# Second FFN pass: the low part of the gated value computed on GpSimd instead of VectorE

## The chip, the cores and the metric

One NeuronCore of a Trainium2 chip runs the whole program. The metric is device time in microseconds (us). The kernel before took 2487.13 us, the median of three runs (2484.39 to 2489.68). A profiled execution of it took 2494.55 us; every row below is from that one, and times in the rows count from the start of its span of 2492.5 us.

The engines: TensorE (PE; its weight loads are PEld), VectorE (DVE), ScalarE (ACT), GpSimd (POOL), and SyncE (SP), which issues most of the transfers.

## The reference, cut to what matters

Two layers of a diffusion block on 1024 tokens of width 1024. The second layer's feed-forward network is where the change is:

```python
def _conv_ffn(h, w_in, conv_w, conv_b, w_out, grid):
    u, g = jnp.split(h @ w_in, 2, axis=-1)          # w_in: 1024 x (2 * 2816)
    g = _dwconv_grid(g, conv_w, conv_b, grid)       # 3x3 depthwise, tokens as a 16 x 64 grid
    return (jax.nn.silu(g) * u) @ w_out             # w_out: 2816 x 1024
...
    fx = _conv_ffn(_modulate(x, norm_g[i, 2], sh2, sc2), ffn_w_in[i], ffn_conv_w[i], ffn_conv_b[i], ffn_w_out[i], grid_x)
    x = x + gt2 * _rms_norm(fx, norm_g[i, 3])
```

## The kernel before, in words

**Precision.** Every float32 matrix product is made of three matmuls. Each operand is split into a high part (rounded to the format that TensorE takes, by ScalarE) and a low part (the value minus its high part, by GpSimd or VectorE): high x high, low x high, high x low. L717, L718 and L719 are such a triple, L1365 to L1367 another.

**The second pass.** The 2816 hidden channels are 22 tiles of 128, `j` = 0 to 21. For each tile TensorE makes seven products of 12 matmuls each, in the order `g1`, `s1`, `s2`, `s4`, `s3`, `g2`, `u2`: sums and differences of halves of the weights, from which gate and up value of all 1024 tokens are put together. VectorE and ScalarE combine them (`keep_a`, `keep_b`, L2843, L2849, L2854). VectorE then adds eight taps of the convolution (L2822), ScalarE applies silu, VectorE multiplies by the up value (`fprod`, L2829, function `f_gate`), ScalarE makes the high part `fa_hi` (L2130) and VectorE the low part `fa_lo` (L2835, function `f_low`). With them TensorE runs `down`: 16 triples (8 output blocks by 2 token halves), one each into one of three banks of PSUM in turn, and VectorE adds each to `y_x` (L2868, function `f_add`). Triple n waits until accumulation n-3 is done.

**The order.** Everything is written out by hand, one instruction stream per engine with semaphores between. TensorE: `products(j)`, then `down(j-1)`. VectorE, in `f_tile(j)`: taps of j-1, gate second half of j, gate product of j-1, up second half of j, low part of j-1, gate first half of j, accumulations of j-1. Tile 0 and 1 are written ahead of the loop, tiles 2 to 13 are a hardware loop, and 14 to 21 are unrolled. In tiles 14 to 19 VectorE also computes half a column of a modulation vector (`last_mod_half`, four instructions of 128x256 into `macc_x`, L2294 and L2297), right before the accumulations.

**GpSimd**, in `parts(j)`, splits the weights of the next tile: the low part of `g1` and of the output weights (`fw_lo`, L3061), the sums `s1`, `s2`, the low of `s1`, the sum `s4`, the lows of `s2` and `s4`, the sum `s3`, then the lows of `s3`, `g2` and `u2` (sums are L3047, lows L3055). When the last low is done, SyncE loads the next tile's weights into `f_raw`.

**The end.** The last tile has an `fa_hi2` of its own, and after its gate product no other work of VectorE lies in between.

Of the kernel before, what the change touches and what calls it, by code (L numbers as in the profile page):

```python
# [17 lines left out]
F32 = mybir.dt.float32  # L18
F32R = mybir.dt.float32r
ALU = mybir.AluOpType  # L20
# [10 lines left out]
FT = DFF // P  # L31
# [111 lines left out]
def build(nc, a):  # L143
    with ExitStack() as ctx:
        sems = {}

        def sem(name):
            if name not in sems:
                sems[name] = ctx.enter_context(nc.semaphore(name))
            return sems[name]  # L150
# [4 lines left out]
        def at(name, offset, shape, dt=F32):  # L155
            return nc.alloc_sbuf_tensor_at(name, shape, dt, offset=base + offset)
# [111 lines left out]
        fprod = at("fprod", WORK + 4096, [P, 2, TX])  # L268
        fa_lo = at("fa_lo", WORK + 4096, [P, 2, TX], F32R)
        keep_a = at("keep_a", WORK + 12288, [P, TH])  # L270
        keep_b = at("keep_b", WORK + 14336, [P, TH])
        fa_hi = at("fa_hi", WORK + 16384, [P, TX], F32R)
# [126 lines left out]
        def scaled_x(n, d):  # L399
# [4 lines left out]
        SECOND = {  # L404
            "tap_done": 8 * FT,
            "acc_ready": FT,
            "silu_done": FT,
            "a_done": FT,
            "a_hi_ready": FT,
            "a_lo_ready": FT,  # L410
            "y_part": 7 * FT,
            "w_out_used": 2 * FT + CREDIT,
# [1770 lines left out]
        def _(dve):  # L2183
# [103 lines left out]
            def last_mod_half(n):  # L2287

                c, h = FT - 1 + n // 2, n % 2
                out = macc_x[c - FT + 1][:]  # L2290
                dve.wait_ge(sem("modw1_in"), 16 * (FT + n))
                for k in range(KH * h, KH * h + KH):
                    if k == 0:
                        ins = dve.tensor_scalar(out, modh[:, 0, :], c_pad[:, 0, 0:1], None, ALU.mult)  # L2294
                    else:
                        dve.wait_ge(sem("mod_sum"), c * 16 + 2 * k)
                        ins = dve.scalar_tensor_tensor(out, modh[:, k % KH, :], c_pad[:, k, 0:1], out, ALU.mult, ALU.add)  # L2297
                    ins.then_inc(sem("mod_sum"), 2)
# [513 lines left out]
            def f_taps(j):  # L2812

                cv = fcv[:, j + FT, :]
                g, ac = grid(bank(BANK_G, TX), "x"), grid(acc[:], "x")
                dve.wait_ge(sem("acc_ready"), j + (SECOND["acc_ready"] + 1))
                for i, (r, c) in enumerate(p1.taps):
                    out, src = tap_views(ac, g, r, c, p1.R, p1.W)
                    if i:
                        dve.wait_ge(sem("tap_done"), j * 8 + (SECOND["tap_done"] + i))  # L2820
                    t = tap_index(r, c)
                    dve.scalar_tensor_tensor(out, src, cv[:, t:t + 1], out, ALU.mult, ALU.add).then_inc(sem("tap_done"), 1)  # L2822

            def f_gate(j, par):

                dve.wait_ge(sem("silu_done"), j + (SECOND["silu_done"] + 1))
                dve.wait_ge(sem("act_moved"), j * 4 + (SECOND["act_moved"] + 4))
                dve.wait_ge(sem("dve_moved"), j * 3 + (SECOND["dve_moved"] + 3))
                dve.tensor_tensor(fprod[:, par, :], acc[:], fprod[:, par, :], ALU.mult).then_inc(sem("a_done"), 1)  # L2829

            def f_low(j, par, last=False):

                dve.wait_ge(sem("a_hi_ready"), j + (SECOND["a_hi_ready"] + 1))
                hi = fa_hi2 if last else fa_hi
                dve.tensor_tensor(fa_lo[:, par, :], fprod[:, par, :], hi[:].bitcast(F32), ALU.subtract).then_inc(sem("a_lo_ready"), 1)  # L2835

            def gate_second(j, first=False):

                dve.wait_ge(sem("w_in_used"), j * 7 + (SECOND["w_in_used"] + done_at(first, "s4")))
                dve.wait_ge(sem("act_moved"), j * 4 + (SECOND["act_moved"] + 3))  # L2840
                if not first:
                    dve.wait_ge(sem("tap_done"), j * 8 + SECOND["tap_done"])
                dve.tensor_tensor(ps[:, BANK_G + 1, :], keep_b[:], ps[:, BANK_B, :], ALU.add).then_inc(sem("dve_moved"), 1)  # L2843

            def up_second(j, par, first=False):

                dve.wait_ge(sem("w_in_used"), j * 7 + (SECOND["w_in_used"] + done_at(first, "s3")))
                dve.wait_ge(sem("act_moved"), j * 4 + (SECOND["act_moved"] + 3))
                dve.tensor_tensor(fprod[:, par, TH:TX], fprod[:, par, TH:TX], ps[:, BANK_A, :], ALU.add).then_inc(sem("dve_moved"), 1)  # L2849

            def gate_first(j):

                dve.wait_ge(sem("w_in_used"), j * 7 + (SECOND["w_in_used"] + 6))
                dve.tensor_tensor(ps[:, BANK_G, :], keep_a[:], ps[:, BANK_C, :], ALU.add).then_inc(sem("dve_moved"), 1)  # L2854
# [16 lines left out]
            def f_tile(j, par, adds=True, mod_half=None):  # L2871

                f_taps(j - 1)
                gate_second(j)
                f_gate(j - 1, 1 - par)
                up_second(j, par)
                f_low(j - 1, 1 - par)
                gate_first(j)
                if mod_half is not None:
                    last_mod_half(mod_half)  # L2880
                if adds:
                    f_add(j - 1)
# [3 lines left out]
            gate_first(0)  # L2886
            f_taps(0)
            f_gate(0, 0)
            f_low(0, 0)
            gate_second(1)  # L2890
            up_second(1, 1)
            gate_first(1)
# [56 lines left out]
        def _(pool):  # L2949
# [57 lines left out]
            for u, (dr, n) in enumerate(units):  # L3007
                if n >= 2:
                    i = x_index[u]
# [7 lines left out]
                for v in ([u - 2] if u < len(units) - 1 else [u - 2, u - 1, u]):  # L3017
                    if v in sec_index:
                        i = sec_index[v]
# [12 lines left out]
            def part_sum(name, j, first=False):  # L3032

                if first and name == "s4":
                    pool.wait_ge(sem("r_p"), 4)
                if first and name == "s3":
                    pool.wait_ge(sem("r_q"), 4)
                if not first:
                    pool.wait_ge(sem("w_in_used"), j * 7 + (SECOND["w_in_used"] + free_at(name) - 7))
                one, two, op = {"s1": (part("u1"), part("u2"), ALU.add), "s2": (p_val["s1"][:], part("g1"), ALU.subtract),  # L3040
                                "s4": (part("g2"), p_val["s2"][:], ALU.subtract), "s3": (part("g1"), part("u1"), ALU.subtract)}[name]
                n = ("s1", "s2", "s4", "s3").index(name)
                if name == "s1":
                    pool.wait_ge(sem("raw_in0"), j * 16 + (SECOND["raw_in0"] + 16))
                else:
                    pool.wait_ge(sem("pool_added"), j * 4 + (SECOND["pool_added"] + n))
                pool.tensor_tensor(p_val[name][:], one, two, op).then_inc(sem("pool_added"), 1)  # L3047

            def part_low(name, j, first=False):

                pool.wait_ge(sem("hi_in"), j * 7 + (SECOND["hi_in"] + made_at(first, name)))
                if name in RAW_PART and not first:
                    pool.wait_ge(sem("w_in_used"), j * 7 + (SECOND["w_in_used"] + free_at(name) - 7))
                src = part(name) if name in RAW_PART else p_val[name][:]
                pool.tensor_tensor(p_lo[name][:], src, p_hi[name][:].bitcast(F32), ALU.subtract).then_inc(sem("lo_in"), 1)  # L3055

            def out_low(j, last=False):

                pool.wait_ge(sem("hi_out"), j + (SECOND["hi_out"] + 1))
                w = int(last)  # L3060
                pool.tensor_tensor(fw_lo[w][:], fw_raw[w][:], fw_hi[w][:].bitcast(F32), ALU.subtract).then_inc(sem("lo_out"), 1)  # L3061

            def parts(j, between=None):

                part_low("g1", j)
                if between is not None:
                    between()
                part_sum("s1", j)
                part_sum("s2", j)
                part_low("s1", j)  # L3070
                part_sum("s4", j)
                part_low("s2", j)
                part_low("s4", j)
                part_sum("s3", j)
                part_low("s3", j)
                part_low("g2", j)
                part_low("u2", j)
# [24 lines left out]
                pool.tensor_tensor(x_lo["t3"][:, k:k + 2, :], x_val["t3"][:, k:k + 2, :], x_hi["t3"][:, k:k + 2, :].bitcast(F32), ALU.subtract)\  # L3102
                    .then_inc(sem("pool_low"), 1)
            parts(1)
            parts(2, lambda: out_low(0))
            with pool.Fori(0, FT // 2 - 2) as i:
                parts(i * 2 + 3, lambda: out_low(i * 2 + 1))
                parts(i * 2 + 4, lambda: out_low(i * 2 + 2))
            parts(FT - 1, lambda: out_low(FT - 3))
            out_low(FT - 2)  # L3110
            out_low(FT - 1, True)

            def residual(h, d):
# [96 lines left out]
```

## Time and profile before

| | |
|---|---|
| median of three runs | 2487.13 us (2484.39 to 2489.68) |
| profiled execution, its own time | 2494.55 us |
| its span | 2492.5 us |
| mean granted TensorE clock | 0.976 |
| TensorE busy | 2354.7 us, 94% |
| VectorE busy | 1742.9 us, 70% |
| ScalarE busy | 815.7 us, 33% |
| GpSimd busy | 875.3 us, 35% |
| `fa_lo` on VectorE (L2835) | 22 instructions, median 2.286 us, 1.221 to 2.364 |

The busy shares are means over stages that have different limits. In the page's 40 slices VectorE stands at 8 to 9 tenths through the second FFN pass (from about 1785 us on), and TensorE at 9. A row of the timeline gives start, duration, engine, line, operation, output and inputs, how many instructions are merged, and in brackets how long the engine sat idle before and what ended that.

### The profile page before, as it was taken

Reading aid. Unit: us, or ns where it says so; the run is one execution under the profiler, and the core shown is the slowest. Engines: PE = TensorE matmul, PEld = TensorE weight load, DVE = VectorE, ACT = ScalarE, POOL = GpSimd, SP = SyncE. Lnnn points to the kernel's source line nnn. Section 1 sums busy time; section 2 is a strip of 40 time slices with the busy share of each in tenths; the row PEclk is TensorE's granted clock in tenths of the full one; section 3 lists DMA queues with packets and bytes.
Section 4 is the critical chain, followed back from the end, with each engine's and each line's share of the span. In section 5 each row is a group of like instructions: output and inputs, shape, how many; then the busy total and the mean of one; then the engine's idle time right before and its main releaser. Section 6 shows DMA issues by size and latency. Waiting matters only on the chain.

```text
span 2492.5 us, 36004 instructions
## 1 busy us (share of the span) xinstructions
PE 2354.7 (94%) x13606; PEld 1926.0 (77%) x13606; DVE 1742.9 (70%) x2193; ACT 815.7 (33%) x1182; POOL 875.3 (35%) x432
## 2 busy tenths in 40 slices
PE   7989999999999999999999989798599999999996
PEld 5557777787777778998889987676378888887784
DVE  4467888888888884553533326615778888899986
ACT  3641111121111226553442233323333333333332
POOL 0012122121221235662221115520555665655552
PEclk9999999999999999999999999899799999999998
DMA  8651211222112344552121258512111111111113
GB/s 348 221 195 76 84 51 75 84 84 84 52 74 84 118 173 162 198 178 102 60 79 62 70 140 232 145 34 87 66 48 54 50 50 50 50 59 67 67 42 135
DMA packets 106689, 255.08 MB, mean 102 GB/s; under 512 B 8929, under 2 KB 62817, under 8 KB 92129
## 3 DMA queue, kind: packets, MB, share of 16 engines
q1 hardware_dynamic: 89024, 228.56, 26.6%
q10 hardware_dynamic: 17568, 25.17, 2.8%
q8 instruction: 69, 1.13, 0.2%
q14 instruction: 28, 0.22, 0.0%
HBM read 223.68 MB, written 30.02 MB: 102 GB/s over the span
## 4 chain that ended last, share of the span: by engine, by line
PE 78%; DVE 12%; ACT 4%; DMA 3%; issue 2%; POOL 1%; SPq 0%; ACTq 0%; DVEq 0%; POOLq 0%
PE ps L717 17%; PE ps L718 16%; PE ps L719 16%; PE ps L1365 4%; PE ps L1367 4%; PE ps L1366 4%; DVE acc L2822 3%; DVE y_x L2868 2%; PE ps L1115 2%; PE ps L1116 2%; PE ps L1117 2%; PE ps L1268 1%; PE ps L819 1%; PE ps L852 1%; PE ps L754 1%
## 5 line engine op out<-in xcount | busy, mean ns | idle before, releaser
L2953 POOL TENSOR_TENSOR w_lo<-raw,w_hi 128x2048 fp32r<-128x2048 f32 x57 | 266.8, 4681 | 653.0 <-ACT w_hi L1604 293.9
L717 PE MATMUL ps<-hx_hi,w_hi 128*128 128x512 f32 x848 | 338.7, 399 | 2.5 <-ACT mix_out_c L1758 1.0
L718 PE MATMUL ps<-hx_hi,w_lo 128*128 128x512 f32 x848 | 331.8, 391 | 0.0
L719 PE MATMUL ps<-hx_lo,w_hi 128*128 128x512 f32 x848 | 331.5, 391 | 0.0
L2333 DVE TENSOR_TENSOR y_x<-y_x,ps 128x1024 f32<-128x1024 f32 x176 | 214.7, 1221 | 63.0 <-PE ps L719 59.5
L2315 DVE SCALAR_TENSOR_TENSOR acc<-ps,fcv,acc 128x945 f32<-128x945 f32 (+2 forms) x176 | 215.0, 1222 | 37.4 <-ACT acc L1648 16.3
L2822 DVE SCALAR_TENSOR_TENSOR acc<-ps,fcv,acc 128x945 f32<-128x945 f32 (+2 forms) x176 | 215.0, 1222 | 18.6 <-ACT acc L2159 2.7
L2868 DVE TENSOR_TENSOR y_x<-y_x,ps 128x512 f32<-128x512 f32 x304 | 205.2, 687 | 14.1 <-PE ps L719 14.0
L717 PEld LDWEIGHTS ps<-hx_hi,w_hi 128*128 128x128 f32 x848 | 160.2, 189 | 40.3 <-DVE hx_lo L2470 2.5
L719 PEld LDWEIGHTS ps<-hx_lo,w_hi 128*128 128x128 f32 x848 | 160.1, 189 | 34.0
L718 PEld LDWEIGHTS ps<-hx_hi,w_lo 128*128 128x128 f32 x848 | 160.3, 189 | 30.6
L2964 POOL TENSOR_TENSOR a_lo<-prod,a_hi 128x1024 fp32r<-128x1024 f32 x22 | 52.9, 2404 | 318.7 <-ACT a_hi L1666 318.7
L2284 DVE SCALAR_TENSOR_TENSOR macc<-modw,c_pad,macc 128x256 f32<-128x256 f32 x280 | 155.5, 627 | 0.0
L717 PE MATMUL ps<-fa_hi,fw_hi 128*128 128x512 f32 x352 | 140.1, 398 | 15.4 <-DVE y_x L2868 7.9
L3055 POOL TENSOR_TENSOR p_s_lo<-p_s_val,p_s_hi 128x512 fp32r<-128x512 f32 x88 | 140.6, 1608 | 30.8 <-ACT p_s_hi L2028 30.8
L1115 PE MATMUL ps<-w_hi,hx_hi 128*128 128x256 f32 x512 | 145.4, 284 | 4.3 <-ACT stage L1885 4.3
L717 PE MATMUL ps<-a_hi,w_hi 128*128 128x512 f32 x352 | 145.5, 413 | 2.5 <-DVE y_x L2333 1.2
L1116 PE MATMUL ps<-w_lo,hx_hi 128*128 128x256 f32 x512 | 144.9, 283 | 0.0
L1117 PE MATMUL ps<-w_hi,hx_lo 128*128 128x256 f32 x512 | 144.8, 283 | 0.0
L719 PE MATMUL ps<-a_lo,w_hi 128*128 128x512 f32 x352 | 138.1, 392 | 0.0
L718 PE MATMUL ps<-a_hi,w_lo 128*128 128x512 f32 x352 | 138.0, 392 | 0.0
L718 PE MATMUL ps<-fa_hi,fw_lo 128*128 128x512 f32 x352 | 137.8, 391 | 0.0
(379 smaller groups left out, 5668.7 us busy)
## 6 DMA issues: line engine op xcount, KB each, us to landing
raw<-in_ffn_w SPq DMA_DIRECT2D x44, 1024.0 KB, 6.6
modw<-in_modw SPq DMA_DIRECT2D x48, 512.0 KB, 7.3
raw<-in_ffn_w SPq DMA_DIRECT2D x44, 512.0 KB, 6.4
f_raw<-in_ffn_w SPq DMA_DIRECT2D x22, 1024.0 KB, 5.0
modw<-in_modw SPq DMA_DIRECT2D x21, 1024.0 KB, 4.8
raw<-in_mlstm_w SPq DMA_DIRECT2D x14, 1024.0 KB, 5.3
fw_raw<-in_ffn_w SPq DMA_DIRECT2D x22, 512.0 KB, 3.7
vch<-v_scr SPq DMA_DIRECT2D x18, 512.0 KB, 4.5
```

What stands on the lines that cost most here:

```text
L717: pe.matmul(out, whi, hhi, start=first, stop=False)
L718: pe.matmul(out, wlo, hhi, start=False, stop=False)
L719: return pe.matmul(out, whi, hlo, start=False, stop=last)
L1115: pe.matmul(out, hi[:, k, t0:t0 + CH], wcol(0, k, 0, 2), start=first, stop=False)
L1116: pe.matmul(out, hi[:, k, t0:t0 + CH], wcol(1, k, 0, 2), start=False, stop=False)
L1117: return pe.matmul(out, lo[:, k, t0:t0 + CH], wcol(0, k, 0, 2), start=False, stop=last)
L2284: ins = dve.scalar_tensor_tensor(macc[:, x, :], modw1[:, k, :], c_pad[:, k, x:x + 1], macc[:, x, :], ALU.mult, ALU.add)
L2315: dve.scalar_tensor_tensor(out, src, cv[:, t:t + 1], out, ALU.mult, ALU.add).then_inc(sem("tap_done"), 1)
L2333: dve.tensor_tensor(y[:, d, :], y[:, d, :], bank(4 + 2 * (d % 2), p.T), ALU.add).then_inc(sem("y_added"), 1)
L2822: dve.scalar_tensor_tensor(out, src, cv[:, t:t + 1], out, ALU.mult, ALU.add).then_inc(sem("tap_done"), 1)
L2868: ins = dve.tensor_tensor(y, y, ps[:, BANK_Y + n % 3, :], ALU.add)
L2953: pool.tensor_tensor(w_lo[:, slot, 0:2048], raw[:, slot, 0:2048], w_hi[:, slot, 0:2048].bitcast(F32), ALU.subtract)\
```

## The change

The subtraction that makes `fa_lo` moves from VectorE's stream into GpSimd's for tiles 0 to 20. It stands there between the sum `s4` and the low of `s2`. For the last tile VectorE keeps it, with one more wait, for GpSimd's part of tile 20.

```diff
             def f_low(j, par, last=False):
 
                 dve.wait_ge(sem("a_hi_ready"), j + (SECOND["a_hi_ready"] + 1))
+                dve.wait_ge(sem("a_lo_ready"), j + SECOND["a_lo_ready"])
...
                 f_gate(j - 1, 1 - par)
                 up_second(j, par)
-                f_low(j - 1, 1 - par)
                 gate_first(j)
...
             f_gate(0, 0)
-            f_low(0, 0)
             gate_second(1)
...
+            def gated_low(j, par):
+
+                pool.wait_ge(sem("a_hi_ready"), j + (SECOND["a_hi_ready"] + 1))
+                pool.tensor_tensor(fa_lo[:, par, :], fprod[:, par, :], fa_hi[:].bitcast(F32), ALU.subtract).then_inc(sem("a_lo_ready"), 1)
+
+            def parts(j, between=None, gated=None):
...
                 part_sum("s4", j)
+                if gated is not None:
+                    gated()
                 part_low("s2", j)
...
-            parts(2, lambda: out_low(0))
+            parts(2, lambda: out_low(0), lambda: gated_low(0, 0))
             with pool.Fori(0, FT // 2 - 2) as i:
-                parts(i * 2 + 3, lambda: out_low(i * 2 + 1))
-                parts(i * 2 + 4, lambda: out_low(i * 2 + 2))
-            parts(FT - 1, lambda: out_low(FT - 3))
+                parts(i * 2 + 3, lambda: out_low(i * 2 + 1), lambda: gated_low(i * 2 + 1, 1))
+                parts(i * 2 + 4, lambda: out_low(i * 2 + 2), lambda: gated_low(i * 2 + 2, 0))
+            parts(FT - 1, lambda: out_low(FT - 3), lambda: gated_low(FT - 3, 1))
             out_low(FT - 2)
+            gated_low(FT - 2, 0)
             out_low(FT - 1, True)
```

VectorE ahead of the loop, from the gate product of tile 0 to the accumulations of tile 0. Before:

```order
L2829 TENSOR_TENSOR fprod_202<-acc_84,fprod_202 128x1024
L2835 TENSOR_TENSOR fa_lo_203<-fprod_202,fa_hi_206 128x1024
L2843 TENSOR_TENSOR ps<-keep_b_205,ps 128x512
L2849 TENSOR_TENSOR fprod_202<-fprod_202,ps 128x512
L2854 TENSOR_TENSOR ps<-keep_a_204,ps 128x512
L2866 COPY y_x_51<-ps 128x512 x16
```

The same place on VectorE in the changed kernel:

```order
L2829 TENSOR_TENSOR fprod_202<-acc_84,fprod_202 128x1024
L2844 TENSOR_TENSOR ps<-keep_b_205,ps 128x512
L2850 TENSOR_TENSOR fprod_202<-fprod_202,ps 128x512
L2855 TENSOR_TENSOR ps<-keep_a_204,ps 128x512
L2867 COPY y_x_51<-ps 128x512 x16
```

Three half-size instructions move ahead by one large one (line numbers are one higher in the changed kernel).

VectorE in tile 14, the first with a modulation half. Before:

```order
L2829 TENSOR_TENSOR fprod_202<-acc_84,fprod_202 128x1024
L2849 TENSOR_TENSOR fprod_202<-fprod_202,ps 128x512
L2835 TENSOR_TENSOR fa_lo_203<-fprod_202,fa_hi_206 128x1024
L2854 TENSOR_TENSOR ps<-keep_a_204,ps 128x512
L2294 TENSOR_SCALAR macc_x0_90<-modh_208,c_pad_220 128x256
L2297 SCALAR_TENSOR_TENSOR macc_x0_90<-modh_208,c_pad_220,macc_x0_90 128x256 x3
L2868 TENSOR_TENSOR y_x_51<-y_x_51,ps 128x512 x16
```

The same place on VectorE in the changed kernel:

```order
L2829 TENSOR_TENSOR fprod_202<-acc_84,fprod_202 128x1024
L2850 TENSOR_TENSOR fprod_202<-fprod_202,ps 128x512
L2855 TENSOR_TENSOR ps<-keep_a_204,ps 128x512
L2294 TENSOR_SCALAR macc_x0_90<-modh_208,c_pad_220 128x256
L2297 SCALAR_TENSOR_TENSOR macc_x0_90<-modh_208,c_pad_220,macc_x0_90 128x256 x3
L2869 TENSOR_TENSOR y_x_51<-y_x_51,ps 128x512 x16
```

Between the up value and the modulation half one instruction is left on VectorE, where there were two.

GpSimd in the last `parts`, which is the order of every tile from 2 on. Before:

```order
L3047 TENSOR_TENSOR p_s2_val_200<-p_s1_val_196,f_raw_201 128x512
L3055 TENSOR_TENSOR p_s1_lo_189<-p_s1_val_196,p_s1_hi_182 128x512
L3047 TENSOR_TENSOR p_s4_val_197<-f_raw_201,p_s2_val_200 128x512
L3055 TENSOR_TENSOR p_s2_lo_193<-p_s2_val_200,p_s2_hi_186 128x512
L3055 TENSOR_TENSOR p_s4_lo_190<-p_s4_val_197,p_s4_hi_183 128x512
```

The same place on GpSimd in the changed kernel:

```order
L3046 TENSOR_TENSOR p_s2_val_200<-p_s1_val_196,f_raw_201 128x512
L3054 TENSOR_TENSOR p_s1_lo_189<-p_s1_val_196,p_s1_hi_182 128x512
L3046 TENSOR_TENSOR p_s4_val_197<-f_raw_201,p_s2_val_200 128x512
L3065 TENSOR_TENSOR fa_lo_203<-fprod_202,fa_hi_206 128x1024
L3054 TENSOR_TENSOR p_s2_lo_193<-p_s2_val_200,p_s2_hi_186 128x512
L3054 TENSOR_TENSOR p_s4_lo_190<-p_s4_val_197,p_s4_hi_183 128x512
```

The low of `s2` and all that follows it on GpSimd now stands behind `fa_lo`, and so behind ScalarE's `fa_hi`.

## Rows read from the trace of the kernel before

**Rows 1.** The page, part 1: busy time by engine.

```profile
PE 2354.7 (94%) x13606; PEld 1926.0 (77%) x13606; DVE 1742.9 (70%) x2193; ACT 815.7 (33%) x1182; POOL 875.3 (35%) x432
```

**Rows 2.** Timeline of VectorE and TensorE, one tile of the loop.

```profile
2033.04 2.28 DVE L2835 TENSOR_TENSOR fa_lo<-fprod,fa_hi 128x1024 fp32r<-128x1024 f32 x1 [0.61 <-ACT fa_hi L2130]
...
2036.91 10.89 DVE L2868 TENSOR_TENSOR y_x<-y_x,ps 128x512 f32<-128x512 f32 x16 [0.99 <-PE ps L719]
...
2036.04 0.39 PE L717 MATMUL ps<-fa_hi,fw_hi 128*128 128x512 f32 x1
```

**Rows 3.** Timeline of GpSimd, the same tile and the next.

```profile
2030.92 2.07 POOL L3047 TENSOR_TENSOR p_s_val<-f_raw,p_s_val 128x512 f32<-128x512 f32 x1 [0.17 <-PE ps L1367]
...
2051.20 1.31 POOL L3055 TENSOR_TENSOR p_g_lo<-f_raw,p_g_hi 128x512 fp32r<-128x512 f32 x1 [8.83 <-ACT p_g_hi L2028]
```

**Rows 4.** Instructions of lines 3061 and 2284: duration in ns, least, median, greatest.

```profile
L3061 POOL TENSOR_TENSOR fw_lo<-fw_raw,fw_hi x22: 2369/2412/2428, 1808.1 to 2439.5; 128x1024 fp32r<-128x1024 f32 x22
...
L2284 DVE SCALAR_TENSOR_TENSOR macc<-modw,c_pad,macc x280: 465/474/2631, 224.4 to 889.5; 128x256 f32<-128x256 f32 x140
```

**Rows 5.** Timeline of VectorE, GpSimd and TensorE in tile 15.

```profile
2243.61 2.29 DVE L2835 TENSOR_TENSOR fa_lo<-fprod,fa_hi 128x1024 fp32r<-128x1024 f32 x1 [0.31 <-ACT fa_hi L2130]
...
2246.42 4.37 DVE L2297 SCALAR_TENSOR_TENSOR macc_x<-modh,c_pad,macc_x 128x256 f32<-128x256 f32 x4
2250.70 10.59 DVE L2868 TENSOR_TENSOR y_x<-y_x,ps 128x512 f32<-128x512 f32 x16
...
2243.52 1.29 POOL L3047 TENSOR_TENSOR p_s_val<-f_raw,p_s_val 128x512 f32<-128x512 f32 x1
2244.77 3.71 POOL L3055 TENSOR_TENSOR p_s_lo<-p_s_val,p_s_hi 128x512 fp32r<-128x512 f32 x2
...
2247.85 0.39 PE L717 MATMUL ps<-fa_hi,fw_hi 128*128 128x512 f32 x1
```

**Rows 6.** TensorE's waits, 2190 to 2390 us: sum, times, longest (us).

```profile
PE ps L717 <- DVE y_x L2868: 7.9, 6, 1.4
```

**Rows 7.** Timeline of VectorE: accumulations of the loop's last tile and of tile 20.

```profile
2187.08 3.41 DVE L2868 TENSOR_TENSOR y_x<-y_x,ps 128x512 f32<-128x512 f32 x5 [0.97 <-PE ps L719]
...
2407.15 10.89 DVE L2868 TENSOR_TENSOR y_x<-y_x,ps 128x512 f32<-128x512 f32 x16 [2.31 <-PE ps L719]
```

**Rows 8.** Timeline of VectorE, GpSimd and TensorE in tile 1, ahead of the loop.

```profile
1814.78 1.80 DVE L2829 TENSOR_TENSOR fprod<-acc,fprod 128x1024 f32<-128x1024 f32 x1 [10.07 <-ACT acc L2123]
...
1815.73 2.01 POOL L3047 TENSOR_TENSOR p_s_val<-f_raw,p_s_val 128x512 f32<-128x512 f32 x1 [0.22 <-PE ps L1367]
...
1817.97 0.39 PE L1367 MATMUL ps<-x_lo,p_g_hi 128*128 128x512 f32 x1
1821.31 0.50 PE L1365 MATMUL ps<-t_hi,p_u_hi 128*128 128x512 f32 x1 [2.94 <-DVE fprod L2849]
...
1824.70 0.63 PE L1366 MATMUL ps<-t_hi,p_u_lo 128*128 128x512 f32 x1
```

**Rows 9.** Timeline of VectorE and GpSimd at 571 us, in the first pass.

```profile
571.51 2.62 DVE L2284 SCALAR_TENSOR_TENSOR macc<-modw,c_pad,macc 128x256 f32<-128x256 f32 x1
...
571.45 2.40 POOL L2964 TENSOR_TENSOR a_lo<-prod,a_hi 128x1024 fp32r<-128x1024 f32 x1 [13.46 <-ACT a_hi L1666]
```

**Rows 10.** Timeline of TensorE: the first matmul behind each of two stalls.

```profile
1148.17 0.36 PE L1115 MATMUL ps<-w_hi,hx_hi 128*128 128x256 f32 x1 [2.06 <-ACT stage L1885]
...
1507.10 0.38 PE L1268 MATMUL ps<-vch,dmat 128*128 128x129 f32 x1 [2.03 <-DMA vch<-v_scr]
```

**Rows 11.** Busy time by engine in short stretches; PEclk is behind the five engines.

```profile
1148.20:1152.00 3.80, 3.80 (x32) 3.80 (x33) 0.00 (x0) 1.18 (x4) 2.77 (x1) 1.00 0.37 113
...
1509.00:1511.00 2.00, 2.00 (x16) 1.77 (x16) 0.00 (x0) 0.00 (x0) 0.16 (x1) 0.50 1.04 272
...
1823.00:1825.50 2.50, 2.50 (x7) 1.98 (x6) 0.00 (x0) 0.10 (x1) 0.00 (x0) 0.50 0.00 0
...
2251.00:2256.00 5.00, 4.56 (x20) 3.80 (x21) 5.00 (x9) 0.69 (x2) 3.52 (x3) 1.00 0.11 21
```

More of the change, by code:

```diff
@@ L3061, in out_low @@
                 pool.tensor_tensor(fw_lo[w][:], fw_raw[w][:], fw_hi[w][:].bitcast(F32), ALU.subtract).then_inc(sem("lo_out"), 1)
-            def parts(j, between=None):
+            def gated_low(j, par):
+                pool.wait_ge(sem("a_hi_ready"), j + (SECOND["a_hi_ready"] + 1))
+                pool.tensor_tensor(fa_lo[:, par, :], fprod[:, par, :], fa_hi[:].bitcast(F32), ALU.subtract).then_inc(sem("a_lo_ready"), 1)
+            def parts(j, between=None, gated=None):
                 part_low("g1", j)
```

## The prediction

> **What bounds the kernel now.** I read the page's totals first: TensorE is busy for 94% of the span [rows 1], so a VectorE instruction taken away is worth something only where TensorE waits for VectorE. The change touches the second FFN pass alone, from about 1785 us to the end, so I then read that stretch engine by engine, in order of time. It has four different parts.
>
> *The loop (tiles 2 to 13).* VectorE starts its 16 accumulations 0.99 us after it could have, because TensorE is not there yet [rows 2], and TensorE runs without a stall from tile to tile: accumulations start at 2187.08 us in the loop's last tile [rows 7], and five tiles earlier at 2036.91 us [rows 2], 30.03 us a tile. TensorE sets the time here.
>
> *The six tiles 14 to 19*, in which VectorE also does half a column of the modulation (four small `macc_x` instructions). The accumulations wait for VectorE here: TensorE stalls once in each of the six tiles, 7.9 us in sum, 1.4 us at most [rows 6], and each tile takes about 31.7 us. From 2187.08 to 2407.15 us [rows 7] there are seven tiles in 220.07 us, where seven TensorE-bound ones would take 210.2: 9.9 us are lost, 1.65 for each of six tiles.
>
> *The start (tile 1).* TensorE stalls 2.94 us before the product `u2`, until VectorE has run L2849 [rows 8]. That instruction is queued behind the removed one.
>
> *The end (tile 21)*. Its low part stays on VectorE, and nothing there changes.
>
> **Part 1: the low part on GpSimd in the loop, cost 0.** Removed from VectorE: one instruction of 2.29 us per tile [rows 2], from a queue that waits for TensorE anyway. Added on GpSimd: the nearest rows are its own 128x1024 subtractions, `fw_lo` x22 at 2.37 to 2.43 us [rows 4], and a first-pass one at 2.40 [rows 9]; I take 2.41. GpSimd is at the end of the sum `s4` at 2030.92+2.07 = 2032.99 us [rows 3], and `fa_hi` is ready just before 2033.04, where VectorE started [rows 2]. So `fa_lo` is ready at about 2033.06+2.41 = 2035.47, and TensorE wants it for the matmul that starts at 2036.04 [rows 2], whose weights load some 0.2 us earlier. The cover is 0.3 us. If it is not there, each of 12 tiles costs what is missing; 0 to 0.3 us is the range, 3.6 us in sum. Behind it on GpSimd stand the lows of `s2`, `s4`, `s3`, `g2` and `u2`, about 1.5 us later than now, and behind those on SyncE the load of the next weights. They are hidden by the 8.83 us that GpSimd idles later in each tile [rows 3], and by a tile's lead before TensorE needs them. The added waits hold nothing else.
>
> **Part 2: the start, a gain of 4.5 us.** `fprod` ends at 1814.78+1.80 = 1816.58 us. Without the 128x1024 instruction behind it the two 128x512 ones (0.7 us each) end at about 1818.0 instead of shortly before 1821.3, and TensorE's product `g2` ends at about 1818.2 [rows 8]: the stall of 2.94 us goes. A second thing goes with it. Behind the stall eight matmuls run at a pitch of 0.43 us where 0.23 is usual (1824.70 is one [rows 8]), granted clock 0.50, 1.2 GHz instead of 2.4: 8 x 0.2 = 1.6 us. What is late next is `down` of tile 0, which needs `fa_lo`. GpSimd ends its sum at 1815.73+2.01 = 1817.74, so `fa_lo` is there at 1820.15 and TensorE asks at 1820.9 [rows 8]. 2.9 + 1.6 = 4.5. Bounds: 2.9 (the clock falls all the same) and 4.5.
>
> **Part 3: the six modulation tiles, a loss of 6.2 us.** At first sight 2.29 us leave VectorE where it is the bound, which would give back all 9.9 us. The rows say otherwise. Two instructions that both read two SBUF operands, one on VectorE and one on GpSimd, do not run together here. VectorE's 128x256 instruction at 571.51 us took 2.62 us where the median of its kind is 0.474 [rows 4], since GpSimd had started a 128x1024 one at 571.45, which took 2.40 [rows 9]: it ran when GpSimd had finished. The other way round, `fa_lo` takes 2.29 on VectorE and GpSimd's two lows take 3.71 instead of 2.6 [rows 5]. They take turns, one whole instruction each. Instructions that read PSUM (L2843, L2849, L2854, L2868) always take their 0.68.
>
> Now tile 15, before. `fa_lo` ends at 2245.90. The low of `s2` runs behind it, and the four `macc_x` instructions start at 2246.42. The first waits for the rest of the low of `s2`, the second for the low of `s4`, the third for the sum `s3`, the fourth finds GpSimd idle: 4.37 us in all, a turn costing 1.44. Accumulations start at 2250.70 [rows 5].
>
> After. GpSimd ends the sum `s4` at 2243.52+1.29 = 2244.81 as now and starts `fa_lo`, which holds it to 2244.77+2.41 = 2247.18. VectorE has nothing to do in between except L2849 and L2854, and L2854 needs the product `g2`, which ends 2.7 us before `down` starts at 2247.85 [rows 5], so at 2245.1. L2854 ends at about 2246.0, and the first `macc_x` has to wait until 2247.18. Then come four turns: first `macc_x` to 2247.45, behind the low of `s2` to 2248.9, behind that of `s4` to 2250.3, behind the sum `s3` to 2251.75. Accumulations start at 2251.72, 1.02 us later than now. The tiles that begin with a TENSOR_SCALAR come out the same within 0.05. VectorE stays the bound, each of six tiles grows by 1.03: 6.2 us. `fa_lo` at 2247.2 is still in time for `down`. Bounds: -9.9 (turns cost nothing) and +8.6 (one more turn of 1.44 a tile).
>
> **Part 4: the clock in those tiles, a loss of 6.4 us.** TensorE's six stalls grow from 1.3 to 2.35 us. Stalls of up to 1.4 left the clock at 1.00 [rows 6, 11]; the one of 2.94 was followed by 0.50; that of 2.03 us at 1507.10 was followed by 0.50 as well, that of 2.06 at 1148.17 by 1.00 [rows 10, 11]. So two of the three stalls between 2 and 3 us lowered it. Four of six, at 1.6 us each as in part 2, are 6.4; the bounds are 0 and 9.6. TensorE cannot hide it: behind the stall its 13 triples and VectorE's accumulations have the same pitch, 0.68 and 0.66. The Trainium skill (TensorE: Matmul & The Clock Gate, section "HAM oscillation") has as its rule that only idle gaps longer than any of these lower the clock; by it this part is 0 and the result +1.7. The rows at 1507.10 and 1821.31 go against it. It is the second rival below.
>
> **Sum.** -4.5 + 6.2 + 6.4 = +8.1 us, 0 for the loop. The profiled execution took 2494.55 us (span 2492.5, 2.05 around it), so it would be 2502.7; it was 7.4 us above the median of 2487.13, so against the median I forecast 2495.2.
>
> **Rivals.**
> *VectorE gets its relief after all, faster.* The one mechanism is in the six tiles: the small `macc_x` instructions do not wait for the rest of GpSimd's `fa_lo`, because they get in before it (if GpSimd starts it later than 2246.0) or alongside. Then accumulations start when TensorE is ready, 9.9 us come back and the clock stays: -4.5 - 9.9 = -14.4, 2472.7. It decides from the point where the six tiles lose nothing against now: then -4.5 alone is left, at the edge of what can be told. For it speaks only that VectorE's queue is 2.29 us shorter; against it both pairs of rows [rows 5, 9].
> *The clock does not fall.* -4.5 + 6.2 = +1.7, 2488.8: no change. For it the stall at 1148.17, against it those at 1507.10 and 1821.31.
> *`fa_lo` late in the loop too.* If GpSimd starts it or its signal arrives over 0.3 us late, 12 tiles pay 0.3: +8.1 + 3.6 = +11.7, 2498.8. The cover of 0.3 is thin, but 22 rows of `fw_lo` spread by 0.06 only.
> *The start gives nothing*, since something else holds `down` of tile 0: +12.6, 2499.7. Against it speaks that `fa_lo` has 0.7 us to spare there (part 2).
>
> **How the numbers follow.** My forecast (two falls of the clock or more) has 0.53, the faster rival 0.17, the clock that does not fall (or once) 0.18, `fa_lo` late in the loop 0.07, nothing at the start 0.05. A measurement of this kernel tells 0.2%, 5 us, from no change: below 2482.2 is faster, above 2492.1 slower. Faster: 0.17. Same: 0.18 and a part of my forecast with two falls only, 0.22. Slower: the rest, 0.61. The forecast's own range is 2490 to 2498.5. The given range goes down to 2484 for the clock's rival and up to 2500.5; below it lies the faster rival.
>
> **What the profile after would show.** Right: no stall before `u2` in tile 1; `fa_lo` on GpSimd at 2.4 us; the first `macc_x` of tiles 15, 17 and 19 about 1.5 us long; each tile of the six 32.7 us without a fall of the clock and 34.3 with one; TensorE stalls of 2.3 to 2.4 us; loop tiles still 30.03. Wrong: stalls below 1 us in the six tiles (the turns don't work as I read them), a clock of 1.00 behind stalls of 2.35, or a wait of TensorE for `fa_lo` in the loop.

## The result, and the profile after

The changed kernel takes 2495.97 us (median of 8 runs, 2492.36 to 2498.08), the kernel before 2487.46 us in 8 runs of the same comparison: a ratio of 1.0034, 95% interval 1.0023 to 1.0045. It is 8.5 us slower; 8.1 was forecast. That is a small loss, a third of a per cent, but clear of the scatter.

The profiled execution of the changed kernel has a span of 2491.3 us, 1.2 us *less* than that of before. That is no contradiction. The part ahead of the second pass, which the change doesn't touch, happened to end 9.7 us earlier. So I measure inside the pass, from the matmul with which TensorE goes on in tile 1 after its stall for L2141 (1808.28 us before, 1798.55 after), to the first matmul of `down` of three tiles. The same count for the profiled execution of every kernel, in us:

| kernel | to `down` 0 | to `down` 13 | to `down` 19 | six modulation tiles | median of all runs |
|---|---|---|---|---|---|
| before | 17.27 | 407.95 | 597.99 | 190.04 | 2486.4 to 2487.8 |
| changed | 12.60 | 403.03 | 606.58 | 203.55 | 2495.97 |
| e1_start_only | 12.62 | 403.05 | 592.48 | 189.43 | 2482.45 |
| e2_not_in_mod | 12.64 | 403.08 | 592.51 | 189.43 | 2482.46 |
| e3_mod_only | 17.48 | 407.96 | 612.58 | 204.62 | 2502.62 |
| e4_filled | 13.13 | 403.56 | 599.21 | 195.65 | 2490.12 |
| e5_two_halves | 12.59 | 403.18 | 592.69 | 189.51 | 2481.27 |
| e6_split | 12.61 | 403.04 | 583.24 | 180.20 | 2471.45 |
| e7_split_before | 17.47 | 407.92 | 592.56 | 184.64 | 2480.01 |
| e9_start_split | 12.64 | 403.07 | 587.20 | 184.13 | 2476.35 |
| e10_start_one_three | 12.63 | 403.07 | 583.27 | 180.20 | 2471.87 |
| e11_one_later | 13.63 | 416.10 | 611.82 | 195.72 | 2501.17 |
| e12_unrolled | 12.64 | 403.07 | 606.58 | 203.51 | 2496.22 |

The fifth column is the fourth less the third: the time from `down` 13 to `down` 19. Behind `down` 19 the kernel before takes 86.3 us to the end of the span and the changed one 86.1. So the change gives 4.92 us up to `down` 13 and takes 13.51 in the six modulation tiles: +8.59, and the medians differ by 8.5.

The part behind `down` 19 is not as steady in all the traces. It takes 86.1 to 86.5 us in nine of the thirteen and 88.0 to 88.3 in e2, e3, e4 and e5. All of them have the same stall of TensorE there, 6.65 us, which the change doesn't touch. In it the granted clock falls to 0.50 and stays there for 6.8 us in the nine, for 10.2 in e2, e3 and e5 and for 13.7 in e4. How often that happens in the executions that were not profiled is not known.

The totals of the page, changed kernel (busy time, share of the span, instructions):

```profile
span 2491.3 us, 36023 instructions
...
PE 2353.1 (94%) x13606; PEld 1924.4 (77%) x13606; DVE 1706.8 (69%) x2172; ACT 817.4 (33%) x1182; POOL 906.1 (36%) x453
```

VectorE is 36 us less busy than in [rows 1] and GpSimd 31 us more, and the kernel is slower: the totals of busy time don't show which way it goes.

**The start**, timeline of VectorE, GpSimd and TensorE in tile 1, to be held against [rows 8]:

```profile
1806.79 0.68 DVE L2844 TENSOR_TENSOR ps<-keep_b,ps 128x512 f32<-128x512 f32 x1
1807.39 0.67 DVE L2850 TENSOR_TENSOR fprod<-fprod,ps 128x512 f32<-128x512 f32 x1
...
1812.10 0.69 DVE L2867 COPY y_x<-ps 128x512 f32<-128x512 f32 x1 [2.77 <-PE ps L719]
...
1808.04 2.40 POOL L3065 TENSOR_TENSOR fa_lo<-fprod,fa_hi 128x1024 fp32r<-128x1024 f32 x1
...
1811.15 0.39 PE L717 MATMUL ps<-fa_hi,fw_hi 128*128 128x512 f32 x1
```

The two half-size instructions run right behind `fprod`, TensorE has no stall ahead of `u2`, and no matmul of 0.6 us follows. `fa_lo` ends at 1810.44, in time for `down` at 1811.15.

**The loop**, timeline of the three engines in one tile, against [rows 2]:

```profile
2018.44 2.40 POOL L3065 TENSOR_TENSOR fa_lo<-fprod,fa_hi 128x1024 fp32r<-128x1024 f32 x1
...
2021.38 0.39 PE L717 MATMUL ps<-fa_hi,fw_hi 128*128 128x512 f32 x1
...
2022.26 10.89 DVE L2869 TENSOR_TENSOR y_x<-y_x,ps 128x512 f32<-128x512 f32 x16 [2.70 <-PE ps L719]
```

VectorE now idles 2.70 us where it idled 0.99, and the tile is as long as before.

**The modulation tiles**, timeline in tile 15, against [rows 5]:

```profile
2231.56 0.69 DVE L2855 TENSOR_TENSOR ps<-keep_a,ps 128x512 f32<-128x512 f32 x1 [2.03 <-PE ps L1367]
2232.16 5.79 DVE L2297 SCALAR_TENSOR_TENSOR macc_x<-modh,c_pad,macc_x 128x256 f32<-128x256 f32 x4
2237.87 1.87 DVE L2869 TENSOR_TENSOR y_x<-y_x,ps 128x512 f32<-128x512 f32 x3
...
2230.99 2.40 POOL L3065 TENSOR_TENSOR fa_lo<-fprod,fa_hi 128x1024 fp32r<-128x1024 f32 x1
2233.35 2.91 POOL L3054 TENSOR_TENSOR p_s_lo<-p_s_val,p_s_hi 128x512 fp32r<-128x512 f32 x2
2236.23 1.44 POOL L3046 TENSOR_TENSOR p_s_val<-f_raw 128x512 f32<-128x512 f32 x1
...
2234.08 0.39 PE L717 MATMUL ps<-fa_hi,fw_hi 128*128 128x512 f32 x1
2238.60 0.50 PE L717 MATMUL ps<-fa_hi,fw_hi 128*128 128x512 f32 x1 [2.33 <-DVE y_x L2869]
```

The four `macc_x` take 5.79 us instead of 4.37. Accumulations start 3.79 us behind the first matmul of `down`, 2.85 before. TensorE's waits from 2190 to 2390 us (sum, times, longest) answer to [rows 6]:

```profile
PE ps L717 <- DVE y_x L2869: 13.5, 6, 2.3
```

And the granted clock (PEclk, behind the five engines' busy times) behind the stall of tile 14 and of three later ones answers to [rows 11]:

```profile
2206.00:2211.00 5.00, 5.00 (x22) 4.17 (x23) 5.00 (x8) 0.82 (x2) 3.67 (x3) 1.00 0.11 20
2239.50:2242.00 2.50, 2.50 (x7) 1.93 (x7) 1.62 (x3) 0.00 (x0) 2.50 (x3) 0.50 0.00 0
2273.50:2275.50 2.00, 2.00 (x7) 1.51 (x6) 1.26 (x3) 0.09 (x1) 2.00 (x3) 0.50 0.00 0
2375.70:2378.00 2.30, 2.30 (x7) 1.73 (x7) 1.53 (x3) 0.55 (x2) 2.30 (x3) 0.50 0.00 0
```

At half clock (1.2 GHz) 7 or 8 matmuls run at 0.43 us each. It fell behind five of the six stalls. The tile without a fall takes 32.5 us, the five with one 34.13 to 34.28. One by one, the first `macc_x` of tiles 15, 17 and 19 takes 1.51 us, as forecast, and the fourth of tile 15 takes 1.30 where it took 0.48 before, since GpSimd is no longer idle then.

### The profile page after: what moved, and what is told of

Same layout as the page of the kernel before. It is cut to its first block, busy times and chain, and to the rows that moved or that the text cites. A ratio compares the mean times of both kernels' runs of the same rounds, so it can differ in the third digit from the quotient of the medians.

```text
span 2491.3 us, 36023 instructions
## 1 busy us (share of the span) xinstructions
PE 2353.1 (94%) x13606; PEld 1924.4 (77%) x13606; DVE 1706.8 (69%) x2172; ACT 817.4 (33%) x1182; POOL 906.1 (36%) x453
## 4 chain that ended last, share of the span: by engine, by line
PE 84%; DVE 7%; ACT 3%; DMA 3%; issue 2%; POOL 1%; SPq 0%; ACTq 0%; DVEq 0%; POOLq 0%
PE ps L717 18%; PE ps L719 16%; PE ps L718 16%; PE ps L1365 5%; PE ps L1367 5%; PE ps L1366 5%; PE ps L1115 2%; PE ps L1116 2%; PE ps L1117 2%; PE ps L819 1%; PE ps L1268 1%; DVE macc_x L2297 1%; PE ps L852 1%; PE ps L754 1%; PE ps L1006 1%
## 5 line engine op out<-in xcount | busy, mean ns | idle before, releaser
L717 PE MATMUL ps<-fa_hi,fw_hi 128*128 128x512 f32 x352 | 142.8, 406 | 20.6 <-DVE y_x L2869 13.5
L719 PE MATMUL ps<-fa_lo,fw_hi 128*128 128x512 f32 x352 | 141.4, 402 | 0.0
```

The source lines that it names most:

```text
L717: pe.matmul(out, whi, hhi, start=first, stop=False)
L719: return pe.matmul(out, whi, hlo, start=False, stop=last)
```

## The experiments

Each ratio is against the kernel before, run beside the experiment on the same chip, where its median was 2486.4 to 2487.8 us. Of each edit the lines that matter are shown.

### Where the gain and the loss are: e1_start_only, e2_not_in_mod, e3_mod_only

GpSimd makes the low parts of some tiles, VectorE those of the others, each waiting for the one before. The core of e1, against the kernel before (tile 0 on GpSimd only):

```diff
             f_gate(0, 0)
-            f_low(0, 0)
             gate_second(1)
...
-            parts(2, lambda: out_low(0))
+            parts(2, lambda: out_low(0), lambda: gated_low(0, 0))
```

In e1, e2 and e3 GpSimd's turns for tiles 15 to 20 are also written out instead of looped.

> Only the low part of tile 0 is made on GpSimd; all others stay on VectorE, as before the change. Theory (three separate effects: a start that gains, a loop that costs nothing, six modulation tiles that lose): the stall of 2.94 us before the product u2 in tile 1 and the slow matmuls behind it go, everything later keeps its time, so 4.9 us faster than before, about 2482.5, with the six tiles at 31.7 us each and stalls of 1.25 to 1.4. Rival (the gain at the start is only run-to-run scatter of the part ahead of it, or is given back at the loop): no difference to before, 2487. Rival (removing fa_lo from VectorE in the loop also matters): less than the gain of e2_not_in_mod.

Measured: 2482.45 us against 2486.41, ratio 0.9984 (0.9976 to 0.9993); to `down` 13 it is 4.90 us less than before. The six tiles take 0.6 us less than before as well (189.43), whether from GpSimd's turns being written out or from something else no run shows. The medians differ by 4.0, so not all of what the trace has is in them.

e2 adds the loop's twelve and the last two, but leaves 13 to 18 to VectorE (the line is shown against the changed kernel):

```diff
-                f_tile(j, j % 2, mod_half=j - 14 if j < 20 else None)
+                f_tile(j, j % 2, mod_half=j - 14 if j < 20 else None, low=True if j < 20 else False, mixed=j == 14 or j == 20)
```

> GpSimd makes the low parts of tiles 0 to 12 and of 19 and 20; in the six tiles with a modulation half (low parts 13 to 18) VectorE keeps them. Theory: the loop's 12 moved instructions are worth nothing either way, so the same time as e1_start_only within 1 us, 4.9 us under before, about 2482.5; first macc_x in the six tiles 0.8 us, no stall of TensorE over 1.4 us, no fall of the clock there. Rival (the changed kernel is slow because GpSimd's own work gets later in every tile): this kernel keeps two thirds of that and would stay above before.

Measured: 2482.46 us, ratio 0.9984 (0.9975 to 0.9993). It is equal to e1 in every column of the table within 0.03 us. The twelve low parts of the loop cost and gain nothing, whichever engine makes them.

e3 is the reverse, with GpSimd making 13 to 18 alone (against the kernel before):

```diff
-            with pool.Fori(0, FT // 2 - 2) as i:
+            with pool.Fori(0, 6) as i:
                 parts(i * 2 + 3, lambda: out_low(i * 2 + 1))
                 parts(i * 2 + 4, lambda: out_low(i * 2 + 2))
+            for j in range(15, FT - 1):
+                parts(j, lambda: out_low(j - 2), lambda: gated_low(j - 2, j % 2, j == 15))
             parts(FT - 1, lambda: out_low(FT - 3))
```

> The reverse: GpSimd makes only the low parts 13 to 18, those of the six tiles with a modulation half; the others stay on VectorE. Theory: the stall at the start stays, the six tiles grow from 31.7 to 32.6 us, and to 34.2 where the clock falls: 5.6 us for the turns and 1.58 for each fall, 5 of 6 in the changed kernel's trace, so +13.5 us, about 2500.5 (2497 to 2503 with 3 to 6 falls). Rival (the loss belongs to all tiles with fa_lo on GpSimd): under +6.

Measured: 2502.62 us, ratio 1.0059 (1.0046 to 1.0072), +16.2, at the upper edge of what was expected. The six tiles take 14.6 us more than before, the first 34.0 already: the clock fell behind all six stalls. Another 1.8 us of the profiled execution lie behind `down` 19 (see above). The stalls are even a little shorter than in the changed kernel (TensorE's waits, sum, times, longest):

```profile
PE ps L717 <- DVE y_x L2870: 12.9, 6, 2.2
```

So the loss comes with these six instructions and what they set off.

### What a fall of the clock costs: e4_filled and its control e12_unrolled

```diff
+            def fill(j, n=6):
+
+                pe.wait_ge(sem("dve_moved"), j * 3 + (SECOND["dve_moved"] + 6))
+                for k in range(n):
+                    pe.matmul(ps[:, BANK_C, :], fw_hi[0][:, 0:P], fa_hi[:, 0:TH], start=True, stop=True, skip_group_check=True)
...
+                    if n == 3 and filled:
+                        fill(j)
```

> The changed kernel, with six more matmuls in each of TensorE's down parts 13 to 18, written to a bank that nobody reads then, right where TensorE stalls for the accumulations (ahead of triple 3). They take 6 x 0.23 = 1.4 us of a stall of 2.2 to 2.3 us, so they delay nothing; the stalls become about 0.9 us. Nothing else changes but that the PE's last loop turns are written out. Theory (the long stalls lower the clock and that costs 1.6 us each): granted clock 1.00 through the six tiles, every tile 32.6 to 32.8 us, 7.9 us faster than the changed kernel, about 2488. Rival (tiles of 34.2 us come from something else than the clock, such as the longer GpSimd chain, and the clock is only a symptom): tiles stay at 34.2, 2496.

> The control for e4_filled: TensorE's last loop turns written out as there, but without the six filling matmuls. Theory: the changed kernel's time, 2496, with falls of the clock in five or six of the six tiles. Rival (writing the loop out is what made e4_filled faster): 2490.

Measured: e4 2490.12 us, ratio 1.0012 (1.0004 to 1.0021); e12 2496.22, ratio 1.0037 (1.0023 to 1.005). Their six tiles take 195.65 and 203.51 us: the filling matmuls are worth 7.86 us, and writing the loop out nothing (203.55 in the changed kernel). e12 had five falls, as the changed kernel. e4's waits of TensorE, and its granted clock behind the stall of tile 15 and the one of tile 19:

```profile
PE ps L717 <- DVE y_x L2880: 5.5, 6, 1.0
```

```profile
2243.50:2249.00 5.50, 5.48 (x24) 4.56 (x25) 5.50 (x9) 0.88 (x2) 3.72 (x3) 1.00 0.17 30
2374.00:2380.00 6.00, 6.00 (x26) 4.94 (x27) 5.99 (x10) 0.80 (x2) 3.64 (x3) 1.00 0.23 55
```

With 36 more matmuls the kernel is faster. Without a fall a tile takes 32.54 to 32.70 us, so each of the five falls costs 1.57. What stays is 195.65 - 190.04 = 5.6 us, the turns. The median came out 2 us above the expectation. The profiled execution has 0.5 us more at the start, where two or three more matmuls were slow than in the others, and 2.1 more behind `down` 19, where the clock stayed at 0.50 longer (see above). Neither lies in the six tiles, which came out as forecast. Whether the other executions of e4 have the same two is not known.

### Is it turns, one instruction each? e5_two_halves

```diff
-                pool.tensor_tensor(fa_lo[:, par, :], fprod[:, par, :], fa_hi[:].bitcast(F32), ALU.subtract).then_inc(sem("a_lo_ready"), 1)
+                pool.tensor_tensor(fa_lo[:, par, 0:TH], fprod[:, par, 0:TH], fa_hi[:, 0:TH].bitcast(F32), ALU.subtract)
+                pool.tensor_tensor(fa_lo[:, par, TH:TX], fprod[:, par, TH:TX], fa_hi[:, TH:TX].bitcast(F32), ALU.subtract).then_inc(sem("a_lo_ready"), 1)
```

> The changed kernel, with GpSimd's fa_lo as two instructions of 128x512 in place of one of 128x1024: the same work, more turns. Theory (VectorE waits for the GpSimd instruction that is running, and then has its turn before the next one): the first macc_x gets in between the two halves, all four are done 1.0 us earlier, accumulations start as in the kernel before, TensorE's six stalls are back at 1.2 to 1.4 us, the clock stays at 1.00, the six tiles take 31.7 us. So 5.6 + 7.9 = 13.5 us faster than the changed kernel, about 2482.5. Rival (what counts is how much GpSimd has to do before it idles): the same as the changed kernel, 2496, or a little slower.

Measured: 2481.27 us, ratio 0.9983 (0.9974 to 0.9992), 5.2 us under the kernel before, where the changed kernel is 8.5 above it: 13.7 between the two, 13.5 forecast. Timeline of VectorE and GpSimd in tile 15:

```profile
2229.91 0.69 DVE L2855 TENSOR_TENSOR ps<-keep_a,ps 128x512 f32<-128x512 f32 x1 [2.03 <-PE ps L1367]
2230.51 4.76 DVE L2297 SCALAR_TENSOR_TENSOR macc_x<-modh,c_pad,macc_x 128x256 f32<-128x256 f32 x4
...
2229.34 1.29 POOL L3065 TENSOR_TENSOR fa_lo<-fprod,fa_hi 128x512 fp32r<-128x512 f32 x1
2230.60 1.54 POOL L3066 TENSOR_TENSOR fa_lo<-fprod,fa_hi 128x512 fp32r<-128x512 f32 x1
```

The second half takes 1.54 us instead of 1.29: the first `macc_x` had its turn between the halves. The four are done 1.03 us sooner (4.76 instead of 5.79), the stalls are back at 1.15 to 1.23 us, and the clock stays at 1.00. GpSimd does no less work than in the changed kernel. What the waiting engine pays for is the length of the one instruction ahead of it. e11, below, shows the same from the other side: there the second `macc_x` stands behind the whole `fa_lo` and takes 2.42 us in each of the six tiles, where one behind a GpSimd instruction of 128x512 takes 1.33.

### Where the modulation halves should stand: e6, e7, e9, e10

In e6, e7 and e9 `f_tile` puts two of the four `macc_x` behind the accumulations, where GpSimd idles; e10 puts three there.

```diff
-                if mod_half is not None:
-                    last_mod_half(mod_half)
+                if mod_half is not None and 2:
+                    last_mod_half(mod_half, 0, 2)
                 if adds:
                     f_add(j - 1)
+                if mod_half is not None:
+                    last_mod_half(mod_half, 2, 4)
```

> The changed kernel, with each modulation half cut in two: two of the four macc_x instructions stay ahead of the accumulations, two go behind them, where GpSimd idles. Theory: ahead of the accumulations VectorE waits 2.7 us for TensorE in a loop tile, two turns fit in there (the first ends with GpSimd's fa_lo, the second 1.44 us later), and behind them the other two take 0.5 us each. TensorE is the bound in the six tiles too, 30.0 us each, no stall over 0.7 us and no fall of the clock: 4.9 + 9.9 = 14.8 us faster than the kernel before, about 2472. Rival (VectorE's sum of work is the bound in these tiles, wherever the macc_x stand): 31.5 us or more a tile, 2482.

> The kernel before (all low parts on VectorE), with the modulation halves cut in two as in e6_split. Theory: the first two macc_x end at about the time at which TensorE's first triple of down is ready, since only the rest of one low of GpSimd and the low of s4 are in their way; the two behind the accumulations put the taps off by 0.95 us, which the unrolled tiles have to spare against the loop (0.1 us less for each tap). So the 9.9 us of the six tiles come back without the change: 2476.5; the stall at the start stays. Rival (the change is needed for that, since VectorE has 2.29 us more to do): 1 us or more of the 1.65 a tile stays, 2482 or above.

> e1_start_only (low part of tile 0 on GpSimd, all others on VectorE) with the modulation halves cut in two. Theory (the change is worth its start and nothing else): the same as e6_split within 1 us, about 2472. Rival (GpSimd's low parts help once the halves stand well): slower than e6_split by 2 us or more.

> e9_start_split with one macc_x ahead of the accumulations and three behind them (all low parts but that of tile 0 on VectorE). Theory (e9_start_split lost 0.85 us in each of five tiles only because fa_lo on VectorE pushes the two macc_x ahead of the accumulations 1.1 us past the first triple): with one ahead, accumulations start within 0.3 us of TensorE's first triple, the three behind cost 1.45 us ahead of the taps, which the unrolled tiles can spare; all tiles 30.0 us, so the same as e6_split, 2471.5. Rival (with fa_lo on VectorE these tiles hold too much VectorE work for 30 us, so the change is what makes e6_split good): 2475 or more.

Measured: e6 2471.45 us, ratio 0.994 (0.9927 to 0.9952); e7 2480.01, ratio 0.9975 (0.9966 to 0.9985); e9 2476.35, ratio 0.9965 (0.9951 to 0.9979); e10 2471.87, ratio 0.9937 (0.9924 to 0.9951).

e6 is as forecast: 30.03 us a tile, no stall. Timeline of VectorE and TensorE in tile 15:

```profile
2232.18 3.08 DVE L2298 SCALAR_TENSOR_TENSOR macc_x<-modh,c_pad,macc_x 128x256 f32<-128x256 f32 x2
2235.18 10.68 DVE L2870 TENSOR_TENSOR y_x<-y_x,ps 128x512 f32<-128x512 f32 x16
2245.78 1.07 DVE L2298 SCALAR_TENSOR_TENSOR macc_x<-modh,c_pad,macc_x 128x256 f32<-128x256 f32 x2
...
2234.10 0.39 PE L717 MATMUL ps<-fa_hi,fw_hi 128*128 128x512 f32 x1
```

Two `macc_x` cost 3.08 us beside GpSimd's work and 1.07 where it idles.

e7 and e9 missed: 5.4 of the 9.9 us came back in e7, not all, and e9, for which 2472 was forecast, is 4.9 us slower than e6, as its rival had it. Timeline in tile 16 of e7:

```profile
2264.88 2.30 DVE L2836 TENSOR_TENSOR fa_lo<-fprod,fa_hi 128x1024 fp32r<-128x1024 f32 x1 [0.61 <-ACT fa_hi L2130]
...
2267.69 0.78 DVE L2295 TENSOR_SCALAR macc_x<-modh,c_pad 128x256 f32<-128x256 f32 x1
2268.58 1.33 DVE L2298 SCALAR_TENSOR_TENSOR macc_x<-modh,c_pad,macc_x 128x256 f32<-128x256 f32 x1
2269.84 10.63 DVE L2869 TENSOR_TENSOR y_x<-y_x,ps 128x512 f32<-128x512 f32 x16
...
2267.86 0.39 PE L717 MATMUL ps<-fa_hi,fw_hi 128*128 128x512 f32 x1
```

`fa_lo` ends at 2267.18, later against `down` than in the VectorE-bound tile that I had worked from, so accumulations start 1.98 us behind the first matmul of `down` instead of the 0.9 at which they cost nothing; each tile but the first takes 30.83 to 30.99 us, and 30.74 to 30.88 in e9. e10 bears that reading out. With one `macc_x` ahead (VectorE and TensorE in tile 15) accumulations start 0.88 us behind:

```profile
2231.21 2.29 DVE L2838 TENSOR_TENSOR fa_lo<-fprod,fa_hi 128x1024 fp32r<-128x1024 f32 x1 [0.61 <-ACT fa_hi L2130]
2233.42 0.68 DVE L2857 TENSOR_TENSOR ps<-keep_a,ps 128x512 f32<-128x512 f32 x1
2234.02 0.91 DVE L2298 SCALAR_TENSOR_TENSOR macc_x<-modh,c_pad,macc_x 128x256 f32<-128x256 f32 x1
2235.16 1.37 DVE L2871 TENSOR_TENSOR y_x<-y_x,ps 128x512 f32<-128x512 f32 x2 [0.23 <-PE ps L719]
...
2234.28 0.39 PE L717 MATMUL ps<-fa_hi,fw_hi 128*128 128x512 f32 x1
```

e6 and e10 are equal, 180.20 us for six tiles. The best two kernels are 15 to 16 us faster than before, one with all of GpSimd's low parts and one with tile 0's alone. In these tiles the place of four small instructions decides; the engine of the large one only sets which place is right. So e9's rival holds with two `macc_x` ahead, and no longer with one.

### How much time `fa_lo` has: e11_one_later

```diff
+                part_low("s2", j)
                 if gated is not None:
                     gated()
-                part_low("s2", j)
```

> The changed kernel, with GpSimd's fa_lo one instruction later, behind the low of s2 instead of ahead of it. Theory (the cover for fa_lo in the loop is about 0.3 us, as TensorE's weights for down load 0.2 us ahead of its first matmul): 1.25 us later means 0.9 to 1.0 us more in each loop tile, 30.95 to 31.05 instead of 30.03, 11 to 12 us in all; the six modulation tiles stay within 1.5 us each of the changed kernel. About 2505. Rival (TensorE has more to spare there, since down waits for VectorE's accumulations anyway): loop tiles stay at 30.03, 2496.

Measured: 2501.17 us, ratio 1.0056 (1.004 to 1.0071). TensorE's waits in the loop, 1850 to 2180 us (sum, times, longest):

```profile
PE ps L717 <- POOL fa_lo L3065: 6.2, 10, 0.6
```

Loop tiles take 30.92 to 30.96 us, 0.91 more: of 1.25 us later, about 0.34 are covered, as forecast. The total is 4 us under the expectation, for a reason that I had not seen. The six tiles take 195.72 us, 7.8 less than in the changed kernel, and the clock did not fall once: that is what five falls cost in e4 (7.86). With `fa_lo` late, TensorE's idle time comes in two pieces, 0.75 to 0.87 us ahead of `down` and 1.22 to 1.24 behind its third triple, rather than in one of 2.18 to 2.33. A sum of 1.97 to 2.11 in two pieces left the clock alone, where single stalls of 2.08 to 2.10 were followed by a fall in e3, in the one profiled execution of each.

## Why the prediction was right

- **Part 1, the loop.** Forecast 0 with a cover of 0.3 us. Every tile is 30.03 us, e1 and e2 are equal, and e11 measures the cover as 0.34.
- **Part 2, the start.** Forecast 4.5 us gained. Measured 4.67 to `down` 0 and 4.92 to `down` 13, both above the upper bound of 4.5. Both steps are seen: no stall, no slow matmuls. The stall was 0.2 us larger than it looked: the profile counts its 2.94 us from the modelled end of the matmul before it, but the two matmuls start 1821.31 - 1817.97 = 3.34 us apart, 3.11 more than the usual 0.23. And the last of the eight slow matmuls is the first of `down` 0, which makes 0.2 of the step from 4.67 to 4.92. e1 has this gain too, and its median is 4.0 us under the kernel before.
- **Part 3, the turns.** Forecast 6.2 us lost, 1.03 a tile. Measured 5.6 in six tiles (e4), 0.94 a tile: in tile 15 accumulations start 3.79 us behind the first matmul of `down` where the walk gave 3.87. That VectorE waits for GpSimd's whole instruction is shown by e5, where the wait shrinks with that instruction while the work stays.
- **Part 4, the clock.** Forecast 6.4 us, four falls of 1.6. Measured 7.9, five falls of 1.57 (e4 against e12). This is the term that was mis-sized, in its count: I took two falls in three from three earlier stalls of the kernel before, and here it was 16 in 18 stalls over the changed kernel, e12 and e3. In all three traces the falls come in an unbroken row, 34.13 us apart, which is how long a tile with a fall takes. That would fit one fall leading to the next, but no run tests it. The length of a stall alone doesn't decide: the first of e3, 2.08 us, was followed by a fall, and the first of the changed kernel and of e12, 2.18, was not. The kernel before also has two stalls that the prediction doesn't list, 1.66 us each ahead of 1586.78 and 1596.73 among shorter matmuls, and the clock fell to 0.50 behind both.
- The Trainium skill (TensorE: Matmul & The Clock Gate, section "HAM oscillation") has as its rule that only idle gaps longer than any of these stalls lower the clock. By that rule the result was +1.7 us. The measurement decides against it: stalls of 2.08 to 2.33 us were followed by a fall.
- The rival of a relief for VectorE needed the `macc_x` to get in ahead of `fa_lo` or alongside; the first started at 2232.16, 1.2 us behind the start of `fa_lo` at 2230.99, and ended after it.
- The start of the pass and the six tiles are two effects of opposite sign, -4.9 and +13.5. The sum is closer than its parts, and that is luck: 0.4 more gained at the start and 0.6 less lost to the turns stand against 1.5 more lost to the clock, which leaves 0.5.

## What to carry to other kernels

Before an instruction moves to GpSimd, look at what VectorE does while it runs there: where both instructions read two SBUF operands, as here, a small one waits for the whole large one (2.42 us behind one of 128x1024, 1.33 behind one of 128x512). Cutting it in two, or moving the small ones to where GpSimd idles, gave back more than the change had cost. And where a stall of TensorE grows, price the clock that may fall behind it too; here that was 7.9 us against 5.6 for the stalls' own growth.

## What the runs showed of the hardware that I had not expected

A fall of the clock repeated from tile to tile at the same place (tiles of 34.13 to 34.28 us), while nearly the same idle time in two pieces of 0.8 and 1.2 us left it at 1.00 (e11). Six matmuls without use in a stall of 2.3 us made the kernel faster by 1.57 us for each fall avoided (e4). And with one and the same stall of 6.65 us the clock stayed at 0.50 for 6.8, 10.2 or 13.7 us, and the rest of the program took 1.8 to 2.1 us more where it was over 6.8.
